# Norms turned by a diagonal of token factors, and an earlier first output product in the latent attention

## The reference

```
h  = modulate(rms_norm(x, mlp_norm[0]), shift, scale)      # norm "m0", after the differential attention
x  = x + gate * (relu(h @ w1)**2 @ w2)                      # mlp m0
hk = modulate(rms_norm(x, kv_norm),   sh_kv, sc_kv)         # norm "kv", keys and values of the sparse attention
h  = modulate(rms_norm(x, attn_norm[1]), sh_a, sc_a)        # its queries: same x, other gains
kv = hk @ w_kv ; (compressed keys) ; q = h @ b_w_in ; ...
x  = x + gate * (o @ b_w_out)
h  = modulate(rms_norm(x, mlp_norm[1]), shift, scale)       # norm "m1"
...
q, k, v from low-rank latents; softmax(q k^T) v for 8 heads; x = x + o @ w_o     # latent attention
```

## Time and profile before

| | |
|---|---|
| Median of 3 runs | 1425.49 us (1423.74 to 1425.61) |
| Profiled execution, own time | 1421.12 us |
| Its span | 1419.3 us, mean granted clock of PE 0.968 |
| PE busy | 1314.1 us, 93% |
| DVE busy | 876.9 us, 62% |
| ACT busy | 678.7 us, 48% |
| POOL busy | 170.4 us, 12% |
| DMA | 267.42 MB, 188 GB/s over the span |

### The profile page before, as it was taken

One profiled execution on the slowest core, in us unless ns is written; L12 is line 12 of the kernel. 1 busy time (PEld: TensorE's weight loads), 2 busy tenths in 40 slices (PEclk: granted clock), 3 DMA queues, 4 the chain that ended last, 5 costly groups with the idle time before them and its releaser, 6 DMA issues. The chain is left out here.

```text
span 1419.3 us, 22085 instructions
## 1 busy us (share of the span) xinstructions
PE 1314.1 (93%) x8506; PEld 1136.6 (80%) x8506; DVE 876.9 (62%) x1546; ACT 678.7 (48%) x1184; POOL 170.4 (12%) x172
## 2 busy tenths in 40 slices
PE   6797989999989999899999878999999999899999
PEld 2687889888869865688998775699898777799987
DVE  2768678888675377696445674465555655555443
ACT  2354544334444356354544575464444565554442
POOL 0636101101000000010100121010000101011000
PEclk9889999999989899999999998999999999999999
DMA  9967639899866533259665251378655454376660
GB/s 351 317 211 248 199 104 331 291 326 321 288 194 175 172 117 93 81 159 301 178 194 158 87 184 34 103 193 261 188 171 185 135 178 133 92 206 184 188 178 30
DMA packets 249224, 267.42 MB, mean 188 GB/s; under 512 B 11040, under 2 KB 185376, under 8 KB 248736
## 3 DMA queue, kind: packets, MB, share of 16 engines
q1 hardware_dynamic: 246496, 263.52, 59.7%
q10 hardware_dynamic: 2624, 2.49, 0.5%
HBM read 264.83 MB, written 1.15 MB: 187 GB/s over the span
## 5 line engine op out<-in xcount | busy, mean ns | idle before, releaser
L1545 DVE TENSOR_TENSOR wlo<-wring,whi 128x1024 fp32r<-128x1024 f32 (+1 forms) x376 | 456.9, 1232 | 240.1 <-ACT whi L2607 239.4
L2607 ACT ACTIVATE whi<-wring 128x1024 fp32r<-128x1024 f32 (+1 forms) x376 | 388.8, 1043 | 360.4 <-PE ps_p L549 122.6
L547 PE MATMUL bank<-h_hi,whi 128*128 128x256 f32 x1216 | 351.5, 289 | 5.7 <-DVE h_lo L1699 2.3
L548 PE MATMUL bank<-h_lo,whi 128*128 128x256 f32 x1216 | 347.5, 286 | 0.0
L549 PE MATMUL bank<-h_hi,wlo 128*128 128x256 f32 x1216 | 347.1, 285 | 0.0
L547 PEld LDWEIGHTS bank<-h_hi,whi 128*128 128x128 f32 x1216 | 236.9, 195 | 11.8 <-issue 7.9
L548 PEld LDWEIGHTS bank<-h_lo,whi 128*128 128x128 f32 x1216 | 237.1, 195 | 0.7
L549 PEld LDWEIGHTS bank<-h_hi,wlo 128*128 128x128 f32 x1216 | 236.7, 195 | 0.0
L3244 POOL TENSOR_TENSOR ex<-ex 128x512 f32<-128x512 f32 x64 | 73.0, 1140 | 710.9 <-ACT g_hi L2716 710.9
L1767 DVE TENSOR_TENSOR g_lo<-ex,g_hi 128x512 fp32r<-128x512 f32 x64 | 45.0, 703 | 125.2 <-POOL ex L3244 125.0
L547 PE MATMUL bank<-whi,h_hi 128*128 128x512 f32 (+3 forms) x248 | 99.6, 402 | 14.4 <-DVE h_lo L1666 6.2
(11 more groups left out here) (375 smaller groups left out, 1878.8 us busy)
## 6 DMA issues: line engine op xcount, KB each, us to landing
wring<-in_mlp_w SPq DMA_DIRECT2D x128, 512.0 KB, 5.3
wring<-in_ada_w SPq DMA_DIRECT2D x96, 512.0 KB, 7.2
wring<-in_mlp_w_in SPq DMA_DIRECT2D x64, 512.0 KB, 4.8
wring<-in_mlp_w_out SPq DMA_DIRECT2D x64, 512.0 KB, 4.1
wring<-in_a_w_in SPq DMA_DIRECT2D x24, 512.0 KB, 5.7
wring<-in_moba_w_qkv SPq DMA_DIRECT2D x24, 512.0 KB, 4.4
wring<-in_kv_ada_w SPq DMA_DIRECT2D x16, 512.0 KB, 7.3
wring<-in_w_kv SPq DMA_DIRECT2D x12, 512.0 KB, 4.9
```

Source lines behind the costliest of these rows:

```text
L547: nc.tensor.matmul(out, lh, rh, start=first, stop=False)
L548: nc.tensor.matmul(out, lh, rl, start=False, stop=False)
L1545: v.tensor_tensor(piece_view(wlo, p), raw_view(p), piece_view(whi, p).bitcast(F32), ALU.subtract).then_inc(lo_ready, 1)
L2607: a.activation(piece_view(whi, p), raw_view(p), ACT.Copy).then_inc(hi_ready, 1)
```

## The change

1. `norm` is replaced for m0, kv and m1. ACT squares each half of 512 columns as soon as it is added (`half_squares`, into `arena`, no longer into `ps_s`); POOL adds the two sums; DVE multiplies the 128x128 identity by the token factors (`diagonal`), and PE multiplies the blocks of x itself by this diagonal, which turns and scales in one (`turn_scaled`). `xn` is no longer made by the scaling.
2. Out products before m0 and m1 go tile by tile (`out_end`). After them stand three `keep_warm(12)`, two of them ahead of a tile's turn. The last has a bank of its own as target.
3. The first layer of the mlp starts on the even halves (`half_split`), its last four k blocks wait for the odd ones.
4. kv: tile 0 is turned inside the last `down`; only the keys' operand is made before `w_kv`; the queries' operand is made by DVE and ACT behind the first product of `w_kv`, and `late_columns` too. `late_rows(0)` now stands ahead of tile 1's turn, with a `keep_warm(8)`, and `late_rows(1)` behind it. One weight piece fewer is split ahead of the norm.
5. Latent attention: the sums of keys 4 to 7 are taken before head 1 is weighed, the rotary part of queries 4 to 7 after head 2; the first output piece is used before head 3 is turned, so that the pieces are spread one earlier, and half of the last pair stands before the last mix.

```diff
-    for tag, lo, hi in (("l_o", 0, 2), ("l_o_mid", 2, 3), ("l_o_end", 3, 4)):
+    for tag, lo, hi in (("l_o", 0, 1), ("l_o_next", 1, 2), ("l_o_mid", 2, 3), ("l_o_end", 3, 4)):
...
+            def turn_scaled(name, t):
+                pe.wait_ge(sem("diag_ready"), TT * FAST.index(name) + t + 1)
+                for half in range(2):
+                    for i in range(4):
+                        j = 4 * half + i
+                        last = nc.tensor.matmul(x_turned[t][half][:, i * P:(i + 1) * P], x_res[:, t, j * P:(j + 1) * P],
+                                                diag[:, t, :], start=True, stop=True)
+                    last.then_inc(sem("scaled_turned"), 1)
+            def half_split(name, k):
+                if k in (0, 4):
+                    pe.wait_ge(sem(f"{name}_split"), 2 if k == 0 else 4)
...
-            for c in range(2):
-                token_piece(("a_out", c), out_banks[c], out_of, True)
-            mlp("m0", ada_order[10:22], lambda: gate_rows("m0", 40))
-            for t in range(TT):
-                late_rows(t)
-                if t:
-                    keep_warm(10)
-                pe.wait_ge(sem("normed"), TT * NORMS.index("kv") + t + 1)
-                turn("kv", t)
+            out_end("a_out", out_of, out_banks)
             for t in range(TT):
+                keep_warm(12, ps_p[:, 1, 0:P])
+                turn_scaled("m0", t)
+            keep_warm(12, bank[:, out_banks[1][1], 0:P])
+            def turn_inside(i, k):
+                if (i, k) == (3, 2):
+                    turn_scaled("kv", 0)
+            mlp("m0", ada_order[10:22], lambda: gate_rows("m0", 40), inside=turn_inside)
+            late_rows(0)
+            keep_warm(8)
+            turn_scaled("kv", 1)
+            late_rows(1)
+            by_feature(("w_kv", 0), h_kv, W, ready=lambda k: half_split("kv", k))
+            for t in range(TT):
                 late_columns(t)
...
+            pe.wait_ge(sem("kv_split"), 8)       # ahead of q_pair(0)
...
+            def diagonal(name, t):
+                at = rstd(1, D, (name, t), "halves")
+                rstd_wait()
+                v.tensor_scalar(diag[:, t, :], ident[:, :], rs[:, at:at + 1], math.sqrt(D), ALU.mult, ALU.mult).then_inc(
+                    sem("diag_ready"), 1)
+            def scaled_out(name, key, last, out, gains):
+                keep_ahead("dve", last - 2)
+                for c in range(2):
+                    residual((key, c, "tok", 0), 0, c, True)
+                residual((key, 0, "tok", 1), 1, 0, True)
+                diagonal(name, 0)
+                residual((key, 1, "tok", 1), 1, 1, True)
+                dve.wait_ge(sem("gains_ready"), gains)
+                scaled_even(name, 0, out)
+                diagonal(name, 1)
+                scaled_even(name, 1, out)
+                for t in range(TT):
+                    scaled_odd(name, t, out)
+                keep_ahead("dve", last + 1)
...
+                if eps == "halves":
+                    g_.tensor_scalar(rs[:, at:at + 1], ss[:, at:at + 1], ss[:, at + 1:at + 2], D * EPS, ALU.add,
+                                     ALU.add).then_inc(sem("mean_ready"), 1)
...
             head_turn("mla", 2)
+            mla_mix(2)
             qpe_turns(1)
-            mla_mix(2)
+            lo_banks = {}
+            for i in range(4):
+                out_part(("l_o", 0), "mla_low", h, lo_banks, 0, i)
             head_turn("mla", 3)
...
-            q_rope(1, q_half)
+            k_half = k_sums(1)
             head_weigh("mla", 1)
-            k_half = k_sums(1)
             head_max("mla", 2, mask)
             k_scale(1, k_half)
             head_low("mla", 0, h_hi, h_lo)
             head_weigh("mla", 2)
+            q_rope(1, q_half)
             head_max("mla", 3, mask)
             head_low("mla", 1, h_hi, h_lo)
+            keep_ahead("dve", p0 + 17)
             head_weigh("mla", 3)
...
-                keep_ahead("dve", p0 + 15 + u)
+                keep_ahead("dve", p0 + 16 + u)
```

More of the change, by code:

```diff
@@ L1201, in _ @@
             pe.wait_ge(sem("nsa_low"), 8)
[L1202 to L1203 removed]
+            out_end("b_out", (o_hi, o_lo), o_banks)
+            for t in range(TT):
+                keep_warm(12, ps_p[:, 1, 0:P])
+                turn_scaled("m1", t)
+            keep_warm(12, bank[:, o_banks[1][1], 0:P])
             def turn_first(name, count):
@@ L1219, in turn_second @@
                 return step
[L1221 to L1240, removed]
-                bank_emptied(pe, (key, 0, "tok", 1))
-                turn_x(name, 1, 0)
-                bank_emptied(pe, (key, 1, "tok", 1))
-                turn_x(name, 1, 1)
             mlp("m1", ada_order[26:28], before_last=lambda: gate_rows("m1", 64 + 40), inside=turn_first("l", 12))
@@ new lines, in scaled_even @@
+            def scaled_even(name, t, out, o=0):
+                hi, lo, gn, sh = out
+                f, part = whole(2 * t, o), tile_part(2 * t, 4)
+                dve.wait_ge(sem("scaled_turned"), 4 * FAST.index(name) + 2 * t + 1)
+                for i in range(4):
+                    link(v.tensor_scalar(f[:, i, :], x_turned[t][0][:, i * P:(i + 1) * P], gn[:, i:i + 1], sh[:, i:i + 1],
+                                         ALU.mult, ALU.add))
+                settle()
+                link(v.tensor_copy(hi[part], f))
+                settle()
+                v.tensor_tensor(lo[part], f, hi[part].bitcast(F32), ALU.subtract).then_inc(sem(f"{name}_split"), 1)
@@ new lines, in scaled_odd @@
+            def scaled_odd(name, t, out, o=0):
+                hi, _, gn, sh = out
+                f, part = whole(2 * t + 1, o), tile_part(2 * t + 1, 4)
+                act.wait_ge(sem("scaled_turned"), 4 * FAST.index(name) + 2 * t + 2)
+                for i in range(4):
+                    ins = a.activation(f[:, i, :], x_turned[t][1][:, i * P:(i + 1) * P], ACT.Identity,
+                                       scale=gn[:, 4 + i:5 + i], bias=sh[:, 4 + i:5 + i])
+                ins.then_inc(sem("act_done"), 1)
+                n_act[0] += 1
+                act.wait_ge(sem("act_done"), n_act[0])
+                a.activation(hi[part], f, ACT.Copy).then_inc(sem(f"{name}_high"), 1)
@@ new lines, in scaled_norm @@
+            def scaled_norm(name, out, gains, junk, early, last, beside=None):
+                keep_ahead("act", early)
+                for t in range(TT):
+                    for n in range(2):
+                        half_squares(name, t, n, junk)
+                act.wait_ge(sem("gains_ready"), gains)
+                for t in range(TT):
+                    scaled_odd(name, t, out)
+                    if beside:
+                        beside(t)
+                keep_ahead("act", last + 1)
```

168 lines of the change are left out of this document (91 added, 77 removed).

## The result

The changed kernel takes **1409.57 us** (median of 4 runs, 1408.28 to 1413.62) against 1425.55 us for the kernel before beside it (4 runs, 1423.74 to 1428.24): 16.0 us less, ratio 0.9891, 95% interval 0.9866 to 0.9917. The forecast was 1408, range 1401.5 to 1417.

A forecast was written before the change was run, and what follows sets the result against it. PE, busy 93% of the span, was taken as the bound. Savings of 2.0 (m0), 3.3 (m1), 7.8 (kv) and 4.3 us (latent attention), 17.4 in all, off the median 1425.49 gave 1408 us, range 1401.5 to 1417.

The forecast's parts named there:

- the second piece: In kv, the second w_kv weight piece, rounded by ACT only behind its odd halves, would come 0.4 us late.
- the rival of the moved work: In w_kv, PE waits for work moved to DVE and ACT; up to 6.5 us come back, about 1414.5; chance 0.17.
- Head 4 pays: In the latent attention, ACT rounds the third split piece a piece later, so head 4 waits 0.7 us more beyond 1.18.
- the step sum of the forecast: Latent attention: 2.5 us from head 3's earlier turn plus 2.75 of output product less 0.7 at head 4, 4.55; 4.3 taken.
- The loads give it back: Stages that start earlier just wait longer for weights, as in mlp m0; all shifts given back, 1425 us; chance 0.04.
- The clock falls: The new gaps' PE work, as in m0 and m1, runs at 1.2 GHz: 13.4 us slower, 1439; chance 0.03.
- The gaps give more: Head 4's wait and kv's stall vanish, m0 and m1 gain 2.5 and 4: sum 21.5 us, about 1404; chance 0.14.

The follow-up runs named there:

- The combined version: Changed kernel with weights scaled before piece splits in both attentions, ACT's piece before its small loads ahead of m1, eight warm products in m0, twelve in m1: 1397.49 us.
- The warm products ahead of head 4: Changed kernel with eight warm products put ahead of head 4's turn in the latent attention, DVE's work and wait untouched: 1406.32 us.
- the changed kernel once more: The changed kernel run again with nothing edited, as the base for the other runs: 1410.31 us.
- weights ahead of the pieces: Changed kernel where DVE, for heads 4 to 7 of the latent attention, scales a head's weights before splitting a later weight piece: 1404.56 us.

## Why the prediction was right, and where it was not

Stages in us, each between the same two landmarks on PE in all profiles: "m0" and "m1" from the end of the out product to the gate row behind the mlp, "kv" from there to the compression, "attention" from the turn of queries 0 to 3 to the first turn of x in m2. "Old" are the profiles with the code of before in that part, "new" those with the code of the change.

| part | old | new | by stages | by times | forecast |
|---|---|---|---|---|---|
| m0 | 201.5 (200.7, 201.4, 202.4) | 199.4 (7 profiles, 198.7 to 200.1) | 2.0 | 2.8 with m1 | 2.0 |
| m1 | 188.2 (187.9, 188.5, 188.3) | 185.9 (7 profiles, 185.2 to 188.1) | 2.3 | | 3.3 |
| kv | 56.5 (55.8, 56.8, 56.8) | 48.7 (5 profiles), 50.0 (4 where the clock fell) | 7.8 or 6.5 | 8.0 | 7.8 |
| attention | 78.6 (78.7, 78.6) | 76.4 (7 profiles; an eighth 77.7) | 2.2 | 4.7 | 4.3 |
| sum | | | 14.3 or 13.0 | 15.4 | 17.4 |

The three differences of the times add up to 15.4 us, and the whole was 15.6 in that comparison (1425.9 less 1410.31). That they agree to 0.2 us is chance: each ratio is known to some 3 us to either side, and taken by the ratios the three are 4.7, 4.6 and 8.8, together 18.1. That the parts add up, which the forecast took for granted, holds within that noise and no closer. The stages, which repeat better, give 1 to 3 us less than the whole, and that rest has no place; the means of three old profiles are themselves good to about 1 us. The forecast's sum is 3.1 to 4.4 us above that of the stages, so that 1408 came within 1.6 us of the measured time is partly luck.

**m0, right.** Turn of 16 records in 1.79 us, twelve warm products in 2.67 and the diagonal in 0.28 us against 1.78, 2.68 and 0.25 taken; half a square 0.63 for 0.57. POOL's addition took 0.65 us once and 0.30 the other time, and nobody waits for it, since PE's queue ends last: gap 11.5 for 11.6 forecast.

**m1, the gap nearly right, the term a third too large.** 12.5 us for 12.7 in the first profile, but 12.5 to 15.4 over seven. What varies is the time of ACT's late piece ahead of DVE's additions. That is the stretch of the earlier trace rows which the forecast kept as it was, and it lengthens PE's idle time ahead of the first turn, 0.72 to 1.98 us, and 3.15 with eight warm products; behind the two longest the turn itself ran slow (2.66 and 2.86 us for 1.95). The combined version takes this wait away and shows what is left: 11.5. So the term is mis-sized because it took the start of the additions from one trace: the gap shrank by 2.9 us in the mean, 16.2 to 13.3, where 3.3 was forecast. In mlp m1 PE waited 1.4 us for low parts in place of 0.9, but with m0 and m1 undone it waited 1.3 too, so that half a us was given back there isn't shown.

**kv, right with its pieces.** From the end of down to the first product of w_kv 8.3 us for 17.9; less the 1.8 for the turn moved into down that is 7.8 us for the 8.1 forecast. The difference is the 0.29 us of waiting for the first diagonal, which the forecast had ready in time; the second was waited for 0.53 us where 0.75 was counted. The clock at the start of w_kv is 1.00. `late_columns` costs 1.84, the second piece 0.23 where 0.4 was counted. From w_kv's first product DVE was through with the queries' operand after 29.6 us, where 28.9 was forecast (438 less 409.15), and PE shows no idle stretch from there to the compression: the rival of the moved work, 1414.5, is refuted. Not foreseen was that `late_columns`, which stood in a gap before, can now be followed by a fall of the clock that costs 1.5 us.

**Latent attention, the mechanism right and the size wrong.** Head 3's turn comes 2.4 us earlier against the queries' turn (2.5 forecast) with twelve output records done, and head 4's comes 7.94 us behind it for 7.19 before, 0.75 more (0.7 forecast). The step that failed is "Head 4 pays: ... so 0.7 more wait beyond 1.18". It priced the wait as time only. The idle stretch grew from 1.18 to 1.93 us, the clock fell behind it, and head 5 was 9.03 us behind head 4 for 6.85: 2.2 us. With it the step sum of the forecast, 4.55, becomes 2.35, and 2.2 was measured by the stage. The warm products ahead of head 4 show it. The forecast had read this effect in the rows, behind 2.66 and 3.91 us of idle time, and didn't ask whether 1.9 could do it. The first of these readings is off: in kv the clock was at 0.50 from 411.2 on, behind the 3.74 us of idle time that ended at 410.26, before the stretch of 2.66 began. And what the forecast took as a sign that transposes don't hold the clock doesn't show it, since the clock was down while PE still stood idle, ahead of the eight transposes at 870.27:

```profile
868.60:870.20 1.60, 0.00 (x0) 0.00 (x0) 1.28 (x3) 0.15 (x1) 0.29 (x1) 0.50 0.00 0
```

Nor was the clock safe for the shorter idle stretches that the new order leaves. In the changed kernel once more, the profile with 77.7 us in the table, it fell between heads 2 and 3 behind two of 0.78 and 0.99 us, and head 3's turn came 8.00 us behind head 2's for 6.43. In the eleven other profiles with this order it held there:

```profile
863.00:865.90 2.90, 1.58 (x9) 1.35 (x10) 1.23 (x2) 1.67 (x6) 0.00 (x0) 1.00 0.08 19
866.00:869.30 3.30, 3.30 (x9) 2.59 (x8) 1.05 (x4) 0.16 (x2) 0.00 (x0) 0.50 0.48 141
```

**The other rivals.** "The loads give it back" is refuted for the 2.0 us of m0, but it shows where the gap shrinks further: with eight warm products a gap 1.9 us shorter gave a stage 0.4 us shorter (199.1 for 199.4, mean of three profiles and of seven), while ACT's wait for weights in mlp m0 grew from 82.2 to 85.4 us in the mean of the same profiles. "The clock falls" is refuted as it was put: the clock was 1.00 through both turns in m0 and kv, and in m1 it fell only behind idle time. "The gaps give more" didn't come, but the place it named, head 4's wait, is worth most of what weights ahead of the pieces gave: 2.1 us up to head 4's turn and 2.2 of clock behind it, out of 7.1 in the stage; the rest is the shorter waits of heads 5 to 7.

## What to carry to other kernels

A wait on the busiest engine has two prices, its length and the clock behind it: before an edit lengthens a wait, look for the nearest idle stretch in the trace behind which the clock did fall and one behind which it held, and price the new one by both. Where a consumer waits for a short instruction queued behind a long one that nobody needs yet, swap the two; here one line moved gave 5.8 us by the times (7.1 in its stage) where the whole change gave 16. And shorten a gap only as far as the stage behind it can use: with eight warm products in m0 most of 1.9 us was gone again at the end of the stage, while the wait for loads in it grew.

## What the runs showed of the hardware

- A float32 product that isn't a transpose leaves two records 0.112 us apart, in warm products and turns alike; multiplying by a diagonal costs PE 1.79 us per eight blocks and spares DVE 0.75 us of scaling for 0.28 of a diagonal.
- The clock fell behind the idle stretch of 1.92 or 1.93 us ahead of head 4's turn in all eight profiles that have it, behind 1.85, 1.98, 3.15 and 3.47 us in m1, and, in one profile of twelve, behind 0.78 and 0.99 us close together. It held behind single stretches of 0.8, 1.18, 1.35, 1.49, 1.61 and 2.03 us. 1.85 fell where 2.03 held, so the length of the stretch alone doesn't decide.
- The clock also fell with no idle time of PE in the profile, behind sixteen products of one column each, in four of nine executions.
- The same code ahead of m0, which the change leaves alone, ran from 145 to 175 us at 1.00 in the profile before and at 0.94 or 0.89 in the thirteen others. From the first gate row (at 143 to 146) to the end of the out product it took 42.2, 43.8 or 45.4 us accordingly. With what varies ahead of that, the out product ended between 185.8 and 191.3 us, a spread larger than any part but kv is worth.
